# Mixer A's input projection for head pairs 1 to 7 by 2x2 block products on half of its k pairs, with the attention beside it spread over a unit's chunks

## The reference

```python
h = rmsnorm(x, norm_g)
proj = jnp.einsum('bsd,de->bse', h, w_in)
aq, ak, av, ag, bq, bk, bv, bg = jnp.split(proj, SPLITS, axis=-1)
ya = chunk_relbias_attention(aq, ak, av, rel_bias) * jax.nn.silu(ag)   # 16 heads of 64
yb = swa_sink_gqa(rope(bq), rope(bk), bv, sinks) * jax.nn.silu(bg)     # 16 query heads, 2 kv heads
y = jnp.einsum('bse,ed->bsd', jnp.concatenate([ya, yb], axis=-1), w_out)
return x + y
```

## Time and profile before

| What | Value |
|---|---|
| median of 3 runs | 1624.63 us (1624.28 to 1625.23) |
| profiled execution: span from first to last instruction | 1622.9 us |
| PE busy | 1612.2 us, 99% of the span |
| PEld busy | 1372.5 us, 85% |
| DVE busy | 1126.2 us, 69% |
| ACT busy | 879.3 us, 54% |
| POOL busy | 100.2 us, 6% |
| chain that ended last | PE 97%, DVE 2%, DMA 1% |
| mean granted TensorE clock | 0.998 |

### The profile page before, as it was taken

How to read it: one execution, slowest core, us unless ns; L and a number is a source line. 1 busy time by engine, 2 the same in 40 slices (tenths; PEclk the granted TensorE clock), 3 DMA queues, 4 the chain that set the end, 5 groups by cost and what they waited for, 6 DMA issues and landing times.

```text
span 1622.9 us, 24332 instructions
## 1 busy us (share of the span) xinstructions
PE 1612.2 (99%) x8249; PEld 1372.5 (85%) x8249; DVE 1126.2 (69%) x2563; ACT 879.3 (54%) x1911; POOL 100.2 (6%) x74
## 2 busy tenths in 40 slices
PE   9999999999999999999999999999999999999997
PEld 8888888888888888899988888888888888888997
DVE  7666665566577877888855665666567677788875
ACT  7555555555646666433455555555546466654333
POOL 0000000000121200010000000000002211000000
PEclk9999999999999999999999999999999999999999
DMA  7232222231322322344442232222232323223443
GB/s 253 90 102 104 77 90 90 90 115 58 120 94 91 97 106 91 103 152 155 162 142 79 90 112 93 85 83 90 93 112 74 115 91 100 96 91 117 130 143 117
DMA packets 50014, 174.30 MB, mean 107 GB/s; under 512 B 6496, under 2 KB 10880, under 8 KB 35984
## 3 DMA queue, kind: packets, MB, share of 16 engines
q1 hardware_dynamic: 49472, 172.69, 31.4%
q10 hardware_dynamic: 432, 0.55, 0.1%
q0 software_dynamic: 32, 0.08, 0.0%
HBM read 160.10 MB, written 8.47 MB: 104 GB/s over the span
## 4 chain that ended last, share of the span: by engine, by line
PE 97%; DVE 2%; DMA 1%; issue 0%; SPq 0%; ACT 0%; DVEq 0%
PE ps_proj L605 23%; PE ps_proj L604 23%; PE ps_proj L603 23%; PE ps_t L660 2%; PE ps_o L673 2%; PE ps_s L651 1%; PE ps_s L652 1%; PE ps_o L715 1%; PE ps_s L690 1%; PE ps_o L603 1%; PE ps_o L605 1%; PE ps_o L604 1%; PE ps_t L701 1%; PE ps_o L831 1%; PE ps_proj L831 1%; PE ps_o L827 1%
## 5 line engine op out<-in xcount | busy, mean ns | idle before, releaser
L603 PE MATMUL ps_proj<-act_hi,w_hi 128*128 128x512 f32 x1632 | 642.2, 394 | 0.0
L605 PE MATMUL ps_proj<-act_hi,w_lo 128*128 128x512 f32 x1632 | 638.1, 391 | 0.0
L604 PE MATMUL ps_proj<-act_lo,w_hi 128*128 128x512 f32 x1632 | 637.2, 390 | 0.0
L1313 DVE TENSOR_TENSOR w_lo<-w_raw,w_hi 128x512 fp32r<-128x512 f32 (+1 forms) x528 | 382.7, 740 | 128.7 <-ACT w_hi L925 124.8
L925 ACT ACTIVATE w_hi<-w_raw 128x512 fp32r<-128x512 f32 (+1 forms) x528 | 336.6, 656 | 181.4 <-DVE w_raw L1627 58.3
L605 PEld LDWEIGHTS ps_proj<-act_hi,w_lo 128*128 128x128 f32 x1632 | 306.3, 188 | 66.0
L603 PEld LDWEIGHTS ps_proj<-act_hi,w_hi 128*128 128x128 f32 x1632 | 306.7, 188 | 58.3
L604 PEld LDWEIGHTS ps_proj<-act_lo,w_hi 128*128 128x128 f32 x1632 | 306.8, 188 | 57.8
L925 ACT ACTIVATE probs<-probs,rden 128x128 f32<-128x128 f32 (+3 forms) x128 | 72.1, 563 | 119.2 <-DVE rden L1406 119.2
L991 ACT ACTIVATE probs<-probs,nmax 128x128 f32<-128x128 f32 (+3 forms) x128 | 71.9, 562 | 93.9 <-DVE nmax L1385 90.9
L1313 DVE TENSOR_TENSOR arena<-ps_t,arena 128x512 fp32r<-128x512 f32 (+4 forms) x168 | 85.1, 510 | 43.4 <-ACT arena L925 42.6
(11 more groups left out here) (294 smaller groups left out, 2287.2 us busy)
## 6 DMA issues: line engine op xcount, KB each, us to landing
w_raw<-w SPq DMA_DIRECT2D x107, 1024.0 KB, 4.8
w_raw<-w SPq DMA_DIRECT2D x98, 256.0 KB, 3.6
temp<-temp SPq DMA_DIRECT2D x72, 64.0 KB, 4.1
strips_tables<-ext SPq DMA_DIRECT2D x16, 256.0 KB, 5.8
temp<-xT SPq DMA_DIRECT2D x16, 256.0 KB, 4.2
xs<-xy SPq DMA_DIRECT2D x16, 256.0 KB, 4.3
temp<-xs SPq DMA_DIRECT2D x16, 256.0 KB, 4.0
strips_tables<-ext SPq DMA_DIRECT2D x16, 224.0 KB, 5.7
```

What stands on the lines that cost most here:

```text
L603: pe.matmul(dst, wh, act_hi[:, k, :], start=start, stop=False)
L604: pe.matmul(dst, wh, act_lo[:, k, :], start=False, stop=False)
L605: return pe.matmul(dst, wl, act_hi[:, k, :], start=False, stop=stop)
L1313: return nc.vector.tensor_tensor(dst, src, hi, ALU.subtract)
```

## The change

The tiles of a unit u = 1 to 7 are now worked on in two pairs (query and key, then gate and value). A pair of output tiles takes eight chunks. Four of them ("s") hold two k tiles by two output tiles each, done as seven products of 128x256 by three parts, where POOL first makes four sums of 128x128 weight blocks in place (`sum_w_in`). The other four ("p") hold two k tiles by two output tiles as 12 plain products of 128x512. The order within a pair is p p s s s s p p.

The seven products need four banks for a pair: two for the results and two for parts. They are ps_proj0, ps_proj1, ps_s1 and ps_t1, and the next pair uses them with roles swapped (`in_banks`). So the attention keeps only ps_s0 and ps_t0, its steps are spread over points 0, 1, 3, 4, 6, 7, 9, 10 with the transposes two points later and the values at points 7 and 13. ACT copies a part (`copy_p1`), DVE adds up the parts (`sum_of_products_in`, at points 6 and 14) and takes a pair of tiles with two additions and two multiplications (`take_pair`, at point 8 and at the unit's end). Weight chunks are loaded by 256 KB DMAs in five places and split three (ACT) and two (DVE) chunks ahead.

The sums and differences of activations for the first eight k tiles are made once in each layer, in the stage before unit 1, by ACT (scaling and high parts), POOL (16 sums of 128x256) and DVE (low parts). They take most of the room of xy, so mixer A's result of pairs 0 to 5 goes through DRAM (`keep_y`, and one load of 1.5 MB at the end of the units). Weights are laid out for the pairs on the host.

The diff, cut to its core:

```diff
+IN_SUM_K = 4
+IN_CHUNKS = (("p", 0), ("p", 1), ("s", 0), ("s", 1), ("s", 2), ("s", 3), ("p", 2), ("p", 3))
...
+HI_AHEAD = 3
+LO_AHEAD = 2
+Y_STAGE = 6
+SUM_AT = 6
+SCORES_A = (0, 1, 3, 4, 6, 7, 9, 10)
+TURN_A = tuple(p + 2 for p in SCORES_A)
+PV_A = (7, 13)
+TANH_AT, TURN_V_AT, GATE_AT = 3, 4, 5
+HI_Q_AT, LO_Q_AT, HI_K_AT, LO_K_AT = 10, 11, 11, 12
...
+            def load_in(T, L, u, j):
+                T = T + u * 4
+                sp.wait_ge(w_lo_done, T * PTS + (j - 3))
+                i = j % 8
+                kind, c = IN_CHUNKS[i]
+                t, q = divmod(c if kind == "s" else IN_SUM_K + c, PTS)
+                first = in_place(i).start
+                sp.dma_start(raw_f[:, first:first + PLAIN], w_v[bass.ds((T + (j // 8 * 2 + t)) * P, P), q * PLAIN:(q + 1) * PLAIN]
+                             ).then_inc(in_raw[IN_PLACE[i]], 16)
...
-                with sp.Fori(1, PAIRS) as u:
-                    for s in range(4):
-                        prefetch(T + u * 4, s)
+                with sp.Fori(1, PAIRS - 1) as u:
+                    for j in range(4, 20):
+                        load_in(T, L, u, j)
+                    for par in range(2):
+                        sp.sem_inc(w_in[par], 32)
                     load_strips(L, u)
+                    keep_y(L, u - 1)
...
-                if e >= 2:
-                    pe.wait_ge(biased, e0 + (e - 1))
+                if e >= 1:
+                    pe.wait_ge(biased, e0 + e)
                 n = (i + 1) * P
-                dst = ps_s[e % 2][:, 0:n]
+                dst = ps_s[0][:, 0:n]
...
-                if e >= 2:
-                    pe.wait_ge(pt_done, e0 + (e - 1))
+                if e >= 1:
+                    pe.wait_ge(pt_done, e0 + e)
                 for kt in range(i + 1):
-                    mm = pe.transpose(ps_t[e % 2][:, kt * P:(kt + 1) * P], probs[:, e % 2, kt * P:(kt + 1) * P],
+                    mm = pe.transpose(ps_t[0][:, kt * P:(kt + 1) * P], probs[:, e % 2, kt * P:(kt + 1) * P],
...
+            def sum_products_in(L, pair, i, n):
+                (c1, c2), (pa, pb) = in_banks(pair)
+                (c11, c12), (c21, _) = left_right(c1), left_right(c2)
+                (p1, p6), (p5, p7) = left_right(pa), left_right(pb)
+                h_hi = [left_right(act_hi[:, 2 * n + r, :]) for r in range(2)]
+                h_lo = [left_right(act_lo[:, 2 * n + r, :]) for r in range(2)]
+                t_hi = [left_right(h_sum(0, 2 * n + r)) for r in range(2)]
+                t_lo = [left_right(h_sum(1, 2 * n + r)) for r in range(2)]
+                pe.wait_ge(h_sum_lo, (L * IN_SUM_K + n + 1) * 2)
+                products = ((c11, W12, h_hi[1][0], h_lo[1][0]), (c12, S4, h_hi[1][1], h_lo[1][1]),
+                            (c21, W22, t_hi[1][0], t_lo[1][0]), (p1, W11, h_hi[0][0], h_lo[0][0]),
+                            (p5, S1, t_hi[0][0], t_lo[0][0]), (p6, S2, t_hi[1][1], t_lo[1][1]),
+                            (p7, S3, t_hi[0][1], t_lo[0][1]))
+                for dst, b, hi, lo in products:
+                    first = n == 0 and b in (W11, S1)
+                    last = n == IN_SUM_K - 1 and dst not in (c11, c12, c21)
+                    wh = in_block(hi_f, i, b)
+                    pe.matmul(dst, wh, hi, start=first, stop=False, skip_group_check=True)
+                    pe.matmul(dst, wh, lo, start=False, stop=False, skip_group_check=True)
+                    mm = pe.matmul(dst, in_block(lo_f, i, b), hi, start=False, stop=last, skip_group_check=True)
+                mm.then_inc(in_done, 1)
...
+            def unit_sums(T, L, u, att):
+                for p in range(16):
+                    attend(att, p)
+                    if p == TURN_V_AT:
+                        turn_v(T)
+                    i = p % 8
+                    kind, n = IN_CHUNKS[i]
+                    q = pair_in(L, u, p)
+                    if i == 0:
+                        pe.wait_ge(in_summed, q * 4 + 4)
+                    if i == 2:
+                        pe.wait_ge(rows_added, q * 2 + (2 * L + 2))
+                    pe.wait_ge(w_lo_done, T * PTS + (p + 1))
+                    if kind == "s":
+                        sum_products_in(L, p // 8, i, n)
+                    else:
+                        plain_products_in(p // 8, i, n)
...
+            def scale_h(L, half):
+                if half == 0:
+                    act.wait_ge(h_lo_done, L * KT + KT)
+                    if L > 0:
+                        act.wait_ge(x_stored, 16 * OUT_TILES)
+                for k in range(IN_SUM_K * half, IN_SUM_K * half + IN_SUM_K):
+                    nc.scalar.activation(xy[:, k, :], xy[:, k, :], ACT.Copy,
+                                         scale=gain_sb[:, L * KT + k:L * KT + k + 1]).then_inc(h_scaled, 1)
+            def hi_h_sums(L, n):
+                act.wait_ge(h_summed, (L * IN_SUM_K + n + 1) * 4)
+                if n > 1:
+                    act.wait_ge(h_sum_lo, (L * IN_SUM_K + n) * 2)
+                for j in (2 * n, 2 * n + 1):
+                    copy(h_sum(0, j), xy[:, j, :]).then_inc(h_sum_hi, 1)
...
+            def hi_in(T, L, u, j):
+                i = j % 8
+                kind, n = IN_CHUNKS[i]
+                if kind == "s":
+                    act.wait_ge(in_wsum, (pair_in(L, u, j) * IN_SUM_K + (n + 1)) * 4)
+                else:
+                    act.wait_ge(in_raw[IN_PLACE[i]], raw_count(L, u, j))
+                in_passed(act, L, u, j - 4)
+                copy(hi_f[:, in_place(i)], raw_f[:, in_place(i)]).then_inc(w_hi_done, 1)
...
+            def copy_p1(L, u, p):
+                q = pair_in(L, u, p)
+                in_passed(act, L, u, p // 8 * 8 + 5)
+                act.wait_ge(rows_added, q * 2 + (2 * L + 2))
+                copy(in_w1[:, 0:SEQ // 2], in_banks(p // 8)[1][0][:, 0:SEQ // 2]).then_inc(in_copied, 1)
...
+            def unit_sums(T, L, u, att, g):
+                for p in range(16):
+                    def other():
+                        if isinstance(u, int) and p + HI_AHEAD >= 16:
+                            hi_next(tile0(L) + A_SLOTS, L, p + HI_AHEAD - 16)
+                        else:
+                            hi_in(T, L, u, p + HI_AHEAD)
+                    attend(att, p, other)
+                    if p == TANH_AT:
+                        gate(T - 2, t_gate)
+                    if p == TURN_V_AT:
+                        hi_v_a(att[1])
+                    if p % 8 == SUM_AT:
+                        copy_p1(L, u, p)
+                    if p == HI_Q_AT:
+                        hi_q(lambda: act.wait_ge(proj_free, T + 1), g)
+                    if p == HI_K_AT:
+                        hi_k(lambda: act.wait_ge(proj_free, T + 2))
...
+            def lo_in(T, j):
+                dve.wait_ge(w_hi_done, T * PTS + (j + 1))
+                i = j % 8
+                low(lo_f[:, in_place(i)], raw_f[:, in_place(i)], hi_f[:, in_place(i)].bitcast(F32)).then_inc(w_lo_done, 1)
...
+            def sum_of_products_in(L, u, p):
+                q = pair_in(L, u, p)
+                done = q * 4 + 4
+                (p1, p6), (p5, p7) = (left_right(b) for b in in_banks(p // 8)[1])
+                (w1l, w1r), (w2l, w2r) = left_right(in_w1), left_right(in_w2)
+                dve.wait_ge(in_copied, q + 1)
+                nc.vector.tensor_tensor(w2r, p6, w1l, ALU.add).then_inc(in_summed, 1)
+                dve.wait_ge(in_summed, done + 1)
+                nc.vector.tensor_tensor(w2l, p7, w2r, ALU.add).then_inc(in_summed, 1)
+                nc.vector.tensor_tensor(w1r, p5, w2r, ALU.add).then_inc(in_summed, 1)
+                dve.wait_ge(in_summed, done + 3)
+                nc.vector.tensor_tensor(w2r, p5, w2l, ALU.add).then_inc(in_summed, 1)
+            def take_pair(T, L, u, pair, dsts):
+                q = pair_in(L, u, pair * 8)
+                dve.wait_ge(proj_done, T + (2 * pair + 3))
+                dve.wait_ge(in_summed, q * 4 + 8)
+                rows = list(zip(in_banks(pair)[0], (in_w1, in_w2), dsts))
+                for bank_of, row, (dst, scale) in rows:
+                    nc.vector.tensor_tensor(dst, bank_of[:, :], row, ALU.add).then_inc(rows_added, 1)
+                for n, (bank_of, row, (dst, scale)) in enumerate(rows):
+                    dve.wait_ge(rows_added, q * 2 + (2 * L + n + 3))
+                    nc.vector.scalar_tensor_tensor(out=dst, in0=dst, scalar=scale, in1=rstd[:, :], op0=ALU.mult, op1=ALU.mult
+                                                   ).then_inc(proj_free, 1)
...
+            def unit_sums(T, L, u, att, ab, g, v):
+                for p in range(16):
+                    def other():
+                        if isinstance(u, int) and p + LO_AHEAD >= 16:
+                            lo_next(tile0(L) + A_SLOTS, p + LO_AHEAD - 16)
+                        else:
+                            lo_in(T, p + LO_AHEAD)
+                    if p == PV_A[0]:
```

(33 more changed lines are left out.)

237 lines of the change are left out of this document (181 added, 56 removed).

## The result

The changed kernel takes 1679.68 us (median of 4 runs, 1676.73 to 1681.57), beside 1624.45 for the kernel before: 1.0338 times as long (95% interval 1.0324 to 1.0353). The forecast was 1636; slower was right, the size was not.

What follows compares the result with a forecast made beforehand. PE, 99% busy, was taken as the bound. Span 1622.9 less 25.8 for shorter products, plus 2 x 6.3, 18 and 7 for waits, gave 1634.7; with 1.7 from span to median, 1636 us; range 1606 to 1658.

Steps and rivals of the forecast that it cites:

- What it takes away: PE's s chunks: 2.52 us instead of 2.75, saving 0.23 us each, 25.8 us over 112 chunks.
- Waits 2 and 3: Points 12 and 13: PE waits 0.5 and 0.8 us behind ACT's query and key copies; 18 us over 14 units.
- The rival without them: No waits at points 12 and 13, but the one at point 1 stays: 1611 us, 1615 with port loss; chance 0.27.
- Waits 1 and 4 at point 1: PE waits 0.6 us for the bias behind `take_pair` (units 1: 0.9); POOL's port lock on DVE adds 0.5 a unit.
- Wait 4's choice of 0.5 us a unit for the port: POOL's weight sums block DVE at the shared port: bounds 0 and 1.8 us a unit, 0.5 taken, 7 us in all.
- POOL's 0.45: Each 128x128 weight sum on POOL taken as 0.45 us, between 0.32 and 1.29; 16 us of POOL a unit.
- most falls where DVE has slack: POOL's port blocking mostly meets DVE in slack, except at the unit border and at `take_pair` of point 8.
- DMA ... at nothing: Weight loads have the same volume, at a share of 0.27, and the 1.5 MB back is wanted late: no cost.
- The activations' sums lie beside 22 us of PE: Stage before unit 1: ACT, DVE and POOL's sums cost nothing there; their tail is in unit 1's 0.9 us wait.
- Wait 1 in the B unit, 1.8: Layer's last unit, point 1: two more splits (1.2 us) stand before the bias, so PE waits 1.8 us.
- the 1634.7 of the sum: Forecast span of the whole kernel: 1622.9 - 25.8 + 2 x 6.3 + 18 + 7; median 1.7 above it.

Runs made afterwards that it cites:

- the copies run: Changed kernel with ACT's copies of rotated queries and keys one step later, behind softmax steps 6 and 7's high parts: 1669.62 us, 10.1 less.
- the strips early: Changed kernel with the bias strips' loads issued ahead of the last two weight loads, not behind all of them: 1668.83 us, 10.9 less.
- the other edits: On the changed kernel: first bias step ahead of takeover, B unit's bank wait out, copies later, scalings of h spread; with strips early everywhere, 1654.13 us.
- the kernel without sums: Changed kernel with all six edits, and without POOL's weight sums and any work on the sums of h: 1626.00 us (1.0014 of before).

## Why the prediction was wrong

The forecast was 1636 us and its range ended at 1658; 1679.68 was measured. The terms one by one:

- *What it takes away*: right. 2.51 us for a chunk, foreseen 2.52. From the isolated gap of 262 cycles that the Trainium skill gives (TensorE: Matmul & The Clock Gate, "Back-to-back issue gap") the estimate for 21 products is 2.29 us; the trace of after doesn't agree, at 0.120 us each.
- *Waits 2 and 3*: right in place and size, 0.60 and 0.72 us for 0.5 and 0.8; the copies run shows their cause. The rival without them is refuted.
- *Waits 1 and 4 at point 1*: 0.6 and 0.5 foreseen, 1.06 waited in the middle unit. The sum is right, in part by luck: the port stretches the takeover by 0.56 us, but without the sums the wait fell only by 0.27, since the strips' load, put at nothing, lands just behind. In units 1 the wait was 2.65 and 2.94 us, and 0.9 was foreseen: mis-sized.
- *Wait 4's choice of 0.5 us a unit for the port*: mis-sized. Leaving the sums out gave 17.8 us, not 7. POOL's 0.45 was right (0.46 undisturbed, 222.40 in the timeline), and "most falls where DVE has slack" was the step that failed: POOL's result is itself waited for at point 3, behind data that stood late in SP's queue, and further parts of the loss are at points 9 to 15.
- *"DMA ... at nothing"*: failed. I took the share of 0.27 for cover. The share tells nothing of the queue's order: strips and `keep_y` stand ahead of chunk 4's load, and the strips early gave 10.9 us.
- *"The activations' sums lie beside 22 us of PE"*: failed. The stage is 5.6 us longer and unit 1 3.6 and 6.1 (0.9 a layer taken for the tail); without that work 13.9 us go. DVE was busy 47.72 of 59.72 us there, and 41.27 of 54.14 before. How the cost divides between DVE, ACT and POOL was not separated.
- *Wait 1 in the B unit, 1.8*: the wait was put at point 1. It came before the unit's first scores, 2.03 us, at a bank wait that I had not read past; some of the next products then ran at half clock.
- *The clock*: the sum has no term for it. In the profiled run of after about 30 products ran at half clock, in four stretches, about 6 us in all; before had none among its products.

In places: of the 43.9 us by which the span of 1678.6 exceeds the 1634.7 of the sum, 19.8 are in units 2 to 6 (2.5 each for 0.56), 8.0 in the two units 1, 5.6 in layer 0's first stage, 7.5 in the two units 7, and 2.9 behind (the rest is rounding). Not settled: how the 2.0 us missed in a middle unit divide, since the strips and the sums both act through POOL at point 3, and their gains (10.9 and 17.8) were never tried together without the other edits. Small waits and restarts of 0.1 to 0.4 us at points 10, 13 and 15 were not tried apart, nor was the 3.0 and 4.9 us from the B units on that even the kernel without sums loses.

## What to carry to other kernels

Where PE is 99% busy, a shorter stream on it is worth only as much as its suppliers can keep up with: price a change by removing each supplier's new work in turn, and look first at each place where only one bank or one buffer is left. Follow the load queue in its order, item by item; its busy share says nothing of which load lands last. And before an instruction is moved ahead of another, ask which wait the other was covering.
